# Group B of a two-group attention: query tiles of 2 grid rows by 64 columns against strips of 16 rows by 8 columns

## What is computed

```python
rs = clip(r - 4, 0, 16 - 8)                      # first of 8 key rows
col_start = clip(qcol - 8, 0, 64 - 16)           # first of 16 key columns
s = q @ k_nbhd * scale + rpb[:, drow, dcol]      # -1e30 outside the neighbourhood
p = softmax(concat([s, q @ k_ctx * scale]))
o = p_loc @ v_nbhd + p_ctx @ v_ctx
```

## Time and profile before

| | us |
|---|---|
| three runs | 2513.53, 2516.28, 2517.81 |
| median | 2516.28 |
| span of the profiled execution | 2523.1 |
| `front`, to the barrier | 331.4 |
| `attention` | 331.7 to 643.3 |
| `middle` and the start of `experts` | 643.3 to 830 |

### The profile page before, as it was taken

How to read it: one execution, slowest core, us unless ns; L and a number is a source line. 1 busy time by engine, 2 the same in 40 slices (tenths; PEclk the granted TensorE clock), 3 DMA queues, 4 the chain that set the end, 5 groups by cost and what they waited for, 6 DMA issues and landing times. The chain is left out here.

```text
span 2523.1 us, 38785 instructions
## 1 busy us (share of the span) xinstructions
PE 2364.1 (94%) x12974; PEld 1908.0 (76%) x12974; DVE 1872.7 (74%) x2502; ACT 1505.7 (60%) x1883; POOL 405.9 (16%) x317
## 2 busy tenths in 40 slices
PE   6999989999893899999999999999999999999977
PEld 2989967887782677878777777788888888888862
DVE  3465656776676788888888888786876877777866
ACT  3332247777532777777777767565665665665752
POOL 0110023323221102020202021111210211210310
PEclk8999989999996899999999999999999999999998
DMA  6675363444431989898989898887887877977978
GB/s 227 206 202 153 113 162 89 113 107 100 161 132 70 355 309 369 300 366 311 357 307 360 311 355 303 319 296 258 325 290 253 324 282 260 337 269 265 361 292 323
DMA packets 329901, 649.10 MB, mean 257 GB/s; under 512 B 13842, under 2 KB 50930, under 8 KB 329650
## 3 DMA queue, kind: packets, MB, share of 16 engines
q1 hardware_dynamic: 311282, 581.39, 67.3%
q0 software_dynamic: 18528, 66.50, 7.1%
HBM read 609.12 MB, written 44.65 MB: 259 GB/s over the span
## 5 line engine op out<-in xcount | busy, mean ns | idle before, releaser
L2050 DVE TENSOR_TENSOR w_lo_x<-wring,w_hi_x 128x2048 fp32r<-128x2048 f32 x444 | 1008.7, 2285 | 55.5 <-ACT w_hi_x L1891 27.6
L1891 ACT ACTIVATE w_hi_x<-wring 128x2048 fp32r<-128x2048 f32 x444 | 842.8, 1911 | 49.5 <-DMA wring<-in_w_mlp 47.9
L2262 PE MATMUL psum<-w_hi_x,x_hi_x 128*128 128x512 f32 x992 | 418.6, 422 | 10.5 <-DVE w_lo_x L2050 10.5
L2264 PE MATMUL psum<-w_hi_x,x_lo_x 128*128 128x512 f32 x992 | 389.6, 393 | 0.0
L2263 PE MATMUL psum<-w_lo_x,x_hi_x 128*128 128x512 f32 x992 | 389.0, 392 | 0.0
L1854 POOL TENSOR_TENSOR poolgate_x<-poolgate_x 128x1 f32<-128x1 f32 x61 | 69.7, 1143 | 1257.6 <-DVE y_x L2095 822.4
L2259 PE MATMUL psum<-w_hi_x,x_both_x 128*128 128x512 f32 x640 | 270.9, 423 | 0.0
L2260 PE MATMUL psum<-w_lo_x,x_both_x 128*128 128x512 f32 x640 | 250.7, 392 | 0.0
L2262 PEld LDWEIGHTS psum<-w_hi_x,x_hi_x 128*128 128x128 f32 x992 | 189.4, 191 | 46.3 <-DVE w_lo_x L2050 12.8
L2264 PEld LDWEIGHTS psum<-w_hi_x,x_lo_x 128*128 128x128 f32 x992 | 187.4, 189 | 42.0
L2263 PEld LDWEIGHTS psum<-w_lo_x,x_hi_x 128*128 128x128 f32 x992 | 188.5, 190 | 36.5
(11 more groups left out here) (361 smaller groups left out, 4004.7 us busy)
## 6 DMA issues: line engine op xcount, KB each, us to landing
wring<-in_w_mlp SPq DMA_DIRECT2D x444, 1024.0 KB, 6.5
bias<-bias_d SPq DMA_DIRECT2D x32, 640.0 KB, 8.1
ring<-in_w_in SPq DMA_DIRECT2D x36, 512.0 KB, 4.4
ring<-in_w_ada SPq DMA_DIRECT2D x64, 256.0 KB, 3.7
yg<-y_d SPq DMA_DIRECT2D x32, 512.0 KB, 6.8
qaT<-in_x SPq DMA_DIRECT2D x10, 512.0 KB, 4.0
qaT<-in_w_ada SPq DMA_DIRECT2D x2, 2048.0 KB, 8.0
qbT<-in_w_ada SPq DMA_DIRECT2D x2, 2048.0 KB, 13.0
```

The costliest lines, as they stand in the source:

```text
L1891: act.activation(w_hi[:, u % HI, k, :], ring[:, u % RING, k, :], ACT.Copy).then_inc(hi_done, 1)
L2050: dve.tensor_tensor(w_lo[:, u % LO, k, :], ring[:, u % RING, k, :], w_hi[:, u % HI, k, :].bitcast(F32), ALU.subtract).then_inc(lo_done, 1)
L2262: pe.matmul(bank, hi[:, k, :], w_hi[:, u % HI, k, :], start=(not biased and k == 0), stop=False)
L2264: last = pe.matmul(bank, lo[:, k, :], w_hi[:, u % HI, k, :], start=False, stop=(k == KD - 1))
```

## The change

Group B's tile becomes a strip of 8 grid columns by all 16 rows (128 queries, 8 strips). Its keys lie in the own strip and the two beside it, 3 pieces (2 for strips 0 and 7), the same counts as group A has. Within a strip every head has the same bias for all inner strips, so the bias is built once on chip and stays there in `bias`, in the order: strip before, own strip, strip after, then 256 zeros for the context. `mask` of group B becomes one operation, as in group A.

- In `front`, queries and keys are written in strip order by the access pattern of the same instructions. Values are produced as before, then stored to DRAM and read back in strip order, by 2 stores and 8 loads on POOL's queue. The table in DRAM shrinks to 8 shifted copies (8 DMAs and 2 for its edges, none waiting for another).
- At the start of `attention` SP loads `raw` (1.5 MB) in 16 DMAs; the one for grid row r writes the 8 partitions 8r to 8r+7, 64 runs of 1536 bytes. They stand ahead of `w_out`. POOL adds masks to pieces of 4 heads by 128 keys (512 elements): four additions for tile 0, and more for the other forms while pairs run.
- The order of groups is A, B for tiles 0 to 3 and B, A for tiles 4 to 7. As a strip touches all rows, the read-back of the first mixed rows waits for strip 7's store, and ScalarE's sums of squares move behind the copy of the last product.

```diff
@@ front
+            return by_strips(cols)[:, here.start // GRID_W:here.stop // GRID_W, :, :]
...
-                    act.activation(K.qb[:, j, out_cols(g)], bank, ACT.Copy, scale=HD ** -0.5).then_inc(group_copied, 1)
+                    act.activation(strip_part(K.qb[:, j, :], g), in_rows(bank, g), ACT.Copy, scale=HD ** -0.5).then_inc(group_copied, 1)
...
+            for edge in (0, SHIFT_ROWS - NA_ROWS):
+                pool.dma_start(K.shift_d[:, edge:edge + NA_ROWS, :].rearrange("c r n -> c (r n)"), io["k_zeros"].to_broadcast([STRIP, NA_ROWS * SPAN])).then_inc(shift_stored, 16)
+            for c in range(STRIP):
+                pool.wait_ge(w_low, 2 * c + 3)
+                rpb = raw_ap(io["rpb_b"], STRIP - 1 - c, [[RPB_C, NHB * RPB_R], [1, SPAN]])
+                pool.dma_start(K.shift_d[c, NA_ROWS:NA_ROWS + NHB * RPB_R, :], rpb).then_inc(shift_stored, 16)
+            for n, (first, end) in enumerate(((0, FIRST_LATER), (FIRST_LATER, T))):
+                pool.wait_ge(stage_done, VB_STAGES[n])
+                pool.dma_start(K.vb_d[first * P:end * P, :].rearrange("(t p) n -> p t n", p=P), vb[:, first:end, :]).then_inc(vb_moved, 16)
+            pool.wait_ge(vb_moved, 32)
+            for strip in range(STRIPS):
+                pool.dma_start(vb[:, strip, :], in_strips[strip]).then_inc(vb_moved, 16)
@@ attention, SP
-            load_bias(0, 0, FIRST_ROWS)
-            load_mask_b(0)
-            load_bias(0, 1, FIRST_ROWS)
+            sp.dma_start(mask_b, io["k_mask_b"].rearrange("p (m n) -> p m n", m=3)).then_inc(mask_b_loaded, 16)
+            for r in range(GRID_H):
+                src = raw_ap(K.shift_d, (2 * NA_ROWS - 1 - r) * SPAN, [[SHIFT_ROWS * SPAN, STRIP], [RPB_R * SPAN, NHB], [1, GRID_H * SPAN]])
+                sp.dma_start(raw[r * STRIP:(r + 1) * STRIP, :, :, :].rearrange("c h r n -> c h (r n)"), src).then_inc(raw_loaded, 16)
+            sp.dma_start(ring[:, 0, :, :], w_out[:, :, 0:UNIT]).then_inc(w_out_loaded, 16)
+            sp.wait_ge(edge_done, 3)
+            sp.dma_start(ring[:, 1, :, :], w_out[:, :, UNIT:2 * UNIT]).then_inc(w_out_loaded, 16)
@@ attention, POOL
+            pool.wait_ge(raw_loaded, 16 * GRID_H)
+            for part in range(2):
+                pool.tensor_tensor(in_grid(strip_of(part, 1)), strip_raw(part, 1), in_grid(spread(0)), ALU.add)
+                pool.tensor_tensor(in_grid(strip_of(part, 2)), strip_raw(part, 2), in_grid(spread(0)), ALU.add).then_inc(bias_ready, 1)
@@ attention, VectorE
-                    link(dve.tensor_tensor_reduce(row[:, local:every], flat[:, local:every], zeros, -1.0, -NEG, ALU.add, ALU.min, least_ctx[:, s - NHA:s - NHA + 1]))
-                    dve.tensor_tensor_reduce(row[:, 0:local], flat[:, 0:local], bias[:, s - NHA, 0:local], -1.0, least_ctx[:, s - NHA:s - NHA + 1], ALU.add, ALU.min, least[:, s:s + 1]).then_inc(s_masked, 1)
+                    dve.tensor_tensor_reduce(row, flat[:, 512 - local:512 + CTX], bias[:, head, LA - local:LA + CTX], -1.0, -NEG, ALU.add, ALU.min, least[:, s:s + 1]).then_inc(s_masked, 1)
@@ attention, ScalarE
-                if pair in (ALL // 2 - 4, ALL // 2 - 3):
-                    square_rows(pair - ALL // 2 + 4)
...
+            copy_values(ALL // 2 - 1)
+            for t in range(2):
+                square_rows(t)
             act.wait_ge(squared, 4)
             for t in range(2):
                 act.activation(grp[:, t, 1, :], grp[:, t, 0, :], ACT.Sqrt, bias=K.eps[:, :], scale=1.0 / (NHA * HD)).then_inc(K.group_rms, 1)
-            copy_values(ALL // 2 - 1)
```

More of the change, by code:

```diff
@@ L82, in window_tiles, with by_strips @@
     return max(i - 1, 0), min(i + 1, T - 1) - max(i - 1, 0) + 1
[L85 to L90, removed]
+def by_strips(cols):
+    return cols.rearrange("p (s r c) -> p r s c", r=GRID_H, c=STRIP)
 assert max(window_tiles(i)[1] for i in range(T)) * P == LA
-assert max(neighbour_tiles(i)[1] for i in range(T)) * P == LB
 def split(halves):
@@ L917, in _ @@
             pool.dma_start(sink_in[:, :], io["sink_a"].to_broadcast([P, NHA])).then_inc(sink_loaded, 16)
-            pool.sem_inc(bias_ready, 2)
-            with pool.Fori(0, T) as i:
-                pool.wait_ge(mask_b_loaded, 16 * i + 16)
-                for part in range(2):
-                    pool.wait_ge(bias_loaded[part], 32 * i + 32)
-                    rows = bias[:, HEADS * part:HEADS * part + HEADS, :]
-                    pool.tensor_tensor(rows, rows, mask_b.rearrange("p (a n) -> p a n", a=1).to_broadcast([P, HEADS, LB]), ALU.add).then_inc(bias_ready, 1)
-                pool.wait_ge(bias_ready, 2 * i + 4)
+            pool.memset(bias[:, :, LA:LA + CTX], 0.0)
@@ new lines, in heads, with strip_of, strip_raw, in_grid @@
+            def heads(x, part):
+                return x[:, HEADS * part:HEADS * part + HEADS]
+            def strip_of(part, j):
+                return heads(bias, part)[:, :, j * P:(j + 1) * P]
+            def strip_raw(part, j):
+                return heads(raw, part)[:, :, :, STRIP * j:STRIP * j + STRIP]
+            def in_grid(x):
+                return x.rearrange("p h (r c) -> p h r c", c=STRIP)
+            def spread(m):
+                return mask_b[:, m:m + 1, :].to_broadcast([P, HEADS, P])
@@ new lines, in _ @@
+            for part in range(2):
+                pool.wait_ge(bias_free, part + 1)
+                pool.tensor_tensor(strip_of(part, 2), strip_of(part, 2), spread(2), ALU.add).then_inc(bias_ready, 1)
+            for part in range(2):
+                pool.wait_ge(bias_free, part + 3)
+                link(pool.tensor_copy(strip_of(part, 2), strip_of(part, 1)))
+                pool.tensor_copy(strip_of(part, 1), heads(edge, part)).then_inc(bias_ready, 1)
+            pool.wait_ge(bias_ready, 6)
@@ L1038, in _ @@
             for pair in range(ALL // 2):
-                i, at = divmod(pair, PAIRS)
+                n, a, i, group = of_pair(pair)
                 ahead = pair + 1 < ALL // 2
```

320 lines of the change are left out of this document (149 added, 171 removed).

## The result

| | before | changed |
|---|---|---|
| median, us | 2517.1 (4 runs) | 2485.9 (4 runs, 2477.5 to 2489.4) |
| ratio, 95% interval | | 0.9869 (0.9849 to 0.9889) |
| forecast | | 2487, range 2464 to 2510 |
| profiled execution: span | 2523.1 | 2475.6 |
| attention stage in it | 331.70 to 643.33, 311.6 | 332.70 to 606.35, 273.7 |

What follows compares the result with a forecast made beforehand. TensorE, busy 94% of the span, was taken to set each attention pair's cost by its pieces. A gain of 44.1 less 11.1 at the start and 3.5 at the end gave 29.5 us off 2516.3: 2487, range 2464 to 2510.

Steps and rivals of the forecast that it cites:

- Fewer pieces: Attention, fifth pair to last copy: group B pairs cost what group A's do, 276.8 us become 232.7, saving 44.1.
- 0.6 for the change of group: Attention: the first pair after a change of group takes 0.6 us more; bounds 0.5 to 0.8.
- The rival that pairs don't keep 3.83: Attention, group B pairs: a rhythm of 4.2 us over 48 pairs loses 18 us, giving 2505; chance 0.07.
- The start: Opening of attention: VectorE's first group B mask waits for raw loads and POOL, so the fifth pair begins 11.1 us later.
- The 30 us plus 2.0 of landing: Start of attention: 16 raw loads take 30 us from 333.0, successive ones overlapping in twos, and landing at least 2.0 more.
- some 50 GB/s: Start of attention: DMA rate the next profile would show from 333 to 363 if the forecast was right.
- 6.2 us later: Start of attention: time from VectorE going on to the fifth pair's beginning, 356.15 to 362.35 before, taken as unchanged after.
- The rival of raw in time: Start of attention: raw loads take 7.5 us, at most 20; fifth pair 5.7 us earlier, whole 2470 us; chance 0.25.
- The end: Last copy to next stage: squares, table load and roots follow the copy; 2.1 or 4.2 us later, 3.5 taken.
- POOL's additions and the bias loads: Middle of attention: 16 additions of 5.6 us and 30 loads leave; off the path except at `sinkd` in tile 0.
- The merged masks: Group B pairs: merging removes about 0.5 us of VectorE's work a head, costed at nothing as pairs don't wait for VectorE.
- The front: Front stage: strided writing and the values' trip through DRAM stay hidden, last evacuation exposed 0 to 0.5 us; taken as 0.

Runs made afterwards that it cites:

- late_remainder: The changed kernel with VectorE's addition for the next queries (`ql`) made one pair later: 2473.7 us, ratio 0.9833.
- raw_rows: The changed kernel with raw biases gathered in DRAM in front, then loaded by 16 DMAs to 8 neighbouring partitions each: 2484.5 us, one run.
- raw_staged: The changed kernel with raw biases gathered in DRAM in front, then loaded by one DMA to all 128 partitions: 2481.0 us, ratio 0.9849.
- pieces_only: The kernel before with only group B's keys cut to its own tile and the neighbours: attention stage 300.8 us against 311.6.
- pieces_late: The kernel before with group B's keys cut to own tile and neighbours, and VectorE's `ql` additions moved away from POOL's: stage 273.3 us.
- two_masks: The changed kernel with group B's mask of a head as two VectorE operations again: 2489.0 us, ratio 0.9895.
- no_trip: The changed kernel without the trip of group B's values through DRAM: attention opens at 332.81 us against 332.70, stage 275.7 us.

## Why the prediction was right, and which of its terms were not

The forecast of 2487 against 2485.9 is closer than its parts deserve, and that closeness is luck: one gain was taken too large by 4.7 us, one loss too large by 7 to 12, another by 1.6, so that the stage gained 33 to 38 us where 29.5 were forecast. Between that and the 31.2 of the medians lies what the rest of the kernel scatters.

- **Fewer pieces, 232.7 us forecast, 237.4 measured.** The step was right where it said that a pair costs what its pieces make TensorE do: 3.83 us in both groups, 3.21 with 4 pieces. Mis-sized was "0.6 for the change of group". It measured 0.92 to 0.96 at ten of the 12 changes in tiles 1 to 6 (4.77 against 3.83 at most of them), 0.83 and 0.52 at the other two, and nothing at the last of the stage (3.21). By parts: strip 0 took 15.1 us against 13.9, tiles 1 to 6 194.2 against 191.0, tile 7 28.1 against 27.8. The 0.52 of the row came from a pair of 7 pieces, 5.19 us long, which had more room to cover the lateness of VectorE's list; that this is why it was less is argued, not shown. The upper bound of 0.8 was too low as well. late_remainder shows that all of it is the place of one addition in VectorE's list.
- **The rival that pairs don't keep 3.83** did not come true, in any of the kernels.
- **The start, +11.1 forecast, -0.5 measured in the profile, and up to +4.5.** The mechanism was as put: VectorE's first group B mask waits for the raw loads and two POOL additions, TensorE stands, the clock falls. Two sizes were off. The 30 us plus 2.0 of landing were 23.1 in this execution, and 24.9, 25.3, 27.8 and 28.1 in four others with the same loads. The overlap in twos was about right (92 GB/s alone in raw_rows, which has them to the same partitions). The sign "some 50 GB/s" was not seen: the queue also held `w_out`, and moved 147 GB/s from 334 to 356. And "6.2 us later" was read from a row in which more lay behind the wait: before, both heads' transposes of pair 3, its values and the scores of a 6-piece pair came after 356.15; now the first transposes and the values had been done during the wait, and 3.6 us are left (359.27 to 362.87). With 28.1 us the fifth pair begins at 367.6, 35.1 after the stage's opening, against 30.65 before: +4.5. So the start costs between nothing and 5 us, by when the loads land, and this is the larger part of what the runs of the changed kernel scatter by; that is argued from five traces, not shown run by run.
- **The rival of raw in time** is what raw_staged made true: the fifth pair at 24.1 us after the opening, 6.5 sooner than before, where the rival had 5.7. The point from which it decides: where VectorE waits, the time from the opening to the fifth pair is 7.0 to 7.3 us more than "landed" (23.1 and 30.2, 24.9 and 32.2, 28.1 and 35.1), and where it does not, 24.1 in all; so loads with "landed" up to 17 us cost nothing, where the rival had "at most 20".
- **The end, +3.5 forecast, +1.9 measured.** Four squares, table load and roots after the copy, as put. The lower of the two cases held: store and read-back took little enough that ScalarE's squares began right after the copy (600.32), so nothing waited for the rows.
- **POOL's additions and the bias loads, costed at nothing.** Nearly right for the time before (beside `sinkd` they held three `ql` by 0.5 to 0.8 us; after tile 0 they are 14 additions and 28 loads, not 16 and 30), and wrong as a reading of what the change is worth. With the longer pairs VectorE came to `ql` 4.7 to 7.1 us after POOL's addition began, when it was over or nearly so. With pairs of 3.83 us it comes 1.8 to 3.4 us after, as pieces_only shows: cutting the pieces alone brings the stage 11 us and not 38. The bias built once on chip takes POOL's additions out of the middle of the stage, and that is what lets the shorter pairs show. The new tiles alone were not the whole gain; pieces_late shows the other way out. It is no kernel to use, since on the old tiles the cut leaves out keys that the reference wants, but it says that the collision could also have been gone round: its stage, 273.3 us, is as long as the changed kernel's. No kernel keeps the 7 pieces and leaves out the additions; what they held back before, some 6.5 us in all by the rows of `sinkd` and `ql`, is an estimate of what that alone would bring.
- **The merged masks at nothing**: right inside the groups, 0.3 to 0.6 us at each of 8 changes to group B (two_masks), about 4 us in the stage.
- **The front at nothing**: right (no_trip), and the strided evacuations by ScalarE cost 491 ns where they had cost 490.

The range, 2464 to 2510, was wider than it had to be, but its lower end is what the change gives with its three small waits taken away.

## What to carry to other kernels

When the bound engine's work in a period is cut, ask of everything that was hidden under the old period whether it still is: here POOL's additions, and one VectorE addition that waits for ScalarE, cost 2 to 6 us and 0.9 us each time once the pairs were 3.8 us long and not 5.2. An instruction that prepares the group after the next stands best one step after its input is made, not ahead of the operation that the bound engine wants next. And many loads to a few neighbouring partitions each were slow together here: lay the data out in DRAM while the queue is idle and load it in one piece, or spread each load's partitions.

## What the runs showed of the hardware that I had not expected

- VectorE's addition of 128x512 floats from two SBUF operands took 0.69 us alone and 4.41 beside a POOL addition of 128x2560; one of 128x8 took 0.17 alone and 4.77. A mask operation with one operand in PSUM took 0.88 us either way.
- 16 DMAs of 98 KB each landed within 23.1 to 28.1 us of the first issue when each went to 8 neighbouring partitions, 15.5 when its 8 partitions were four apart (the issuing took 6.5 to 7.3 us, and 11.1), and one DMA of the same 1.57 MB to all 128 within 9.3 to 9.9. With nothing else in the queue the neighbouring ones moved 92 GB/s, and the spread ones 142.
